# Rows of block 0 by selection products, block lists inside block 0, and activations turned inside a down product

## What is computed

```python
logits = (xt @ router_w + router_b)            # 512 x 32
top_val, top_idx = lax.top_k(logits, TOP_K)    # 4 of 32 experts for each token
gate = jax.nn.softmax(top_val, axis=-1)
# token/expert pairs are sorted by expert into groups padded to blocks of 128 rows
hh = xblk @ w1[e] + b1[e]                      # 128 x 1024 @ 1024 x 2048
glu = jnp.minimum(hh[:, :D_FF], SWIGLU_LIMIT)
lin = jnp.clip(hh[:, D_FF:], -SWIGLU_LIMIT, SWIGLU_LIMIT)
act = glu * jax.nn.sigmoid(SWIGLU_ALPHA * glu) * (lin + 1.0)
y = act @ w2[e] + b2[e]                        # 128 x 1024 @ 1024 x 1024
# y times its gate is added to the token's row; out = x_new + g_f * sum
```

## Time and profile before

| | |
|---|---|
| median of 3 runs | 2274.47 us (2274.46 to 2274.99) |
| the profiled execution | 2275.2 us, of which its span is 2273.4 us |
| TensorE busy | 2236.3 us (98% of the span), 10681 instructions |
| VectorE, ScalarE, GpSimd busy | 78%, 54%, 17% |
| the chain that ended last | 95% TensorE |
| DMA | 542.93 MB, mean 239 GB/s |
| granted TensorE clock, mean | 0.998 |

### The profile page before, as it was taken

How to read it: one execution, slowest core, us unless ns; L and a number is a source line. 1 busy time by engine, 2 the same in 40 slices (tenths; PEclk the granted TensorE clock), 3 DMA queues, 4 the chain that set the end, 5 groups by cost and what they waited for, 6 DMA issues and landing times.

```text
span 2273.4 us, 30491 instructions
## 1 busy us (share of the span) xinstructions
PE 2236.3 (98%) x10681; PEld 1829.3 (80%) x10681; DVE 1767.7 (78%) x1652; ACT 1238.2 (54%) x1154; POOL 378.3 (17%) x328
## 2 busy tenths in 40 slices
PE   7999999999999999999999999999999999999997
PEld 3888888888887887888788888888888888888886
DVE  6756665555656676757899999999999999999996
ACT  6322132222225524632777777777777777777774
POOL 3000000000221131101512121121112121212112
PEclk9999999999999999999999999999999999999999
DMA  8322323131321121246899999999999999999994
GB/s 301 121 93 93 103 83 130 59 135 57 103 93 38 38 75 38 59 149 224 314 358 371 373 366 382 382 372 362 386 364 373 371 364 383 377 368 380 378 370 168
DMA packets 135513, 542.93 MB, mean 239 GB/s; under 512 B 16131, under 2 KB 24467, under 8 KB 101390
## 3 DMA queue, kind: packets, MB, share of 16 engines
q1 hardware_dynamic: 123192, 516.30, 60.0%
q0 software_dynamic: 11952, 21.44, 4.0%
q10 hardware_dynamic: 296, 4.21, 0.5%
HBM read 533.79 MB, written 26.38 MB: 246 GB/s over the span
## 4 chain that ended last, share of the span: by engine, by line
PE 95%; DMA 1%; DVE 1%; POOL 1%; issue 1%; ACT 1%; POOLq 0%; SPq 0%; DVEq 0%; ACTq 0%
PE ps L2239 90%; PE ps L2795 1%; PE ps L2807 1%; PE ps L2586 1%; DMA ar<-h_d,ar 1%; POOL list_d L858 1%; DMA ar<-in_ctx 0%; PE ps L2531 0%; PE ps L2477 0%; DMA ar<-in_diff_lambda 0%; PE ps L2351 0%; DVE nmx L1846 0%; ACT hhi L1001 0%; PE ps L2684 0%; PE ps L2604 0%
## 5 line engine op out<-in xcount | busy, mean ns | idle before, releaser
L2239 PE MATMUL ps<-whi,yhi 128*128 128x512 f32 x1072 | 346.5, 393 | 0.1
L2239 PE MATMUL ps<-hhi,yhi 128*128 128x512 f32 x1072 | 342.6, 389 | 0.0
L2063 DVE TENSOR_TENSOR hlo<-raw,hhi 128x2048 fp32r<-128x2048 f32 x132 | 302.5, 2293 | 47.1 <-ACT hhi L1308 47.1
L1308 ACT ACTIVATE whi<-raw 128x2048 fp32r<-128x2048 f32 x132 | 253.4, 1920 | 99.1 <-PE ps L2239 99.1
L2063 DVE TENSOR_TENSOR wlo<-raw,whi 128x2048 fp32r<-128x2048 f32 x132 | 298.9, 2285 | 3.6 <-ACT whi L1308 2.0
L1308 ACT ACTIVATE hhi<-raw 128x2048 fp32r<-128x2048 f32 x132 | 253.1, 1918 | 76.3 <-PE ps L2239 76.3
L1421 DVE TENSOR_TENSOR wlo<-raw,whi 128x2048 fp32r<-128x2048 f32 x56 | 128.2, 2289 | 159.4 <-ACT whi L970 159.4
L2239 PEld LDWEIGHTS ps<-whi,yhi 128*128 128x128 f32 x1072 | 201.2, 188 | 53.9 <-issue 12.1
L2239 PEld LDWEIGHTS ps<-hhi,yhi 128*128 128x128 f32 x1072 | 201.2, 188 | 41.8
L2239 PE MATMUL ps<-whi,hhi 128*128 128x512 f32 x592 | 233.3, 394 | 0.0
L2239 PE MATMUL ps<-whi,hlo 128*128 128x512 f32 x592 | 230.9, 390 | 0.0
(11 more groups left out here) (354 smaller groups left out, 4251.8 us busy)
## 6 DMA issues: line engine op xcount, KB each, us to landing
raw<-in_exp_w SPq DMA_DIRECT2D x264, 1024.0 KB, 7.9
ar<-in_exp_w SPq DMA_DIRECT2D x132, 1024.0 KB, 7.8
raw<-in_w_in SPq DMA_DIRECT2D x44, 1024.0 KB, 5.1
raw<-in_w_mod SPq DMA_DIRECT2D x22, 1024.0 KB, 6.2
raw<-in_w_br_ret SPq DMA_DIRECT2D x8, 1024.0 KB, 5.2
ar<-in_x SPq DMA_DIRECT2D x8, 512.0 KB, 7.3
raw<-in_w_br_diff SPq DMA_DIRECT2D x4, 1024.0 KB, 5.1
raw<-in_w_out SPq DMA_DIRECT2D x4, 1024.0 KB, 9.9
```

The source lines that it names most:

```text
L1308: act.activation(e_whi[j % ESPL], e_raw[s], ACT.Copy).then_inc(e_hi, 1)
L2063: V.tensor_tensor(e_wlo[j % ESPL], e_raw[s], e_whi[j % ESPL].bitcast(F32), ALU.subtract).then_inc(e_lo, 1)
L2239: return pe.matmul(out, lhsT, rhs, start=start, stop=stop, skip_group_check=skip)
```

## The change

It has three parts.

First, the rows of block 0 are no longer gathered. TensorE makes them turned, as `ht` slices (the shifted rows of a token tile, still in SBUF) times the selection matrix: `direct_rows(t, q)`, four fp32 matmuls of 128x128 each, for four tiles and two banks. VectorE shifts tile 3's rows after `choose(3)`. As two of these tiles lie in raw slots 3 and 5, SyncE loads chunks 3 and 5 after the last of these products. The only early gather left is block 1's.

Second, the counts, the code lists, `first_rows` and the turned gates move from before `up(0)` into it (`route(kk)`, called after chunks 0, 2 and 3); bias parts follow chunks 4 to 7. The orders on ScalarE, VectorE and GpSimd are rewritten for it.

Third, `turn_act(i)` stands inside the down product of block i-1, after its third chunk of four, and the last down product goes to banks 2 and 3, its order by chunk first, with `act_high` and `act_low` of the last block by halves.

```diff
@@ SyncE
                 if t == LT - 1:
                     sp.dma_start(b2, a["exp_b2"]).then_inc(b2_loaded, 16)
-                if t == 2:
-                    sp.wait_ge(h2_stored, 16 * 2)
-                    load_w1(0, 0, RSLOTS + 1)
                 sp.wait_ge(n2_done, t + 1)
                 sp.dma_start(h2_d[t * P:(t + 1) * P, :], ht[t]).then_inc(h2_stored, 16)
             load_w1(0, 0, RSLOTS)
             sp.wait_ge(h2_stored, 16 * LT)
+            sp.wait_ge(xt_turned, 2)
             load_w1(0, 0, RSLOTS - 1)
+            load_w1(0, 0, RSLOTS + 1)
@@ GpSimd
-            list_tile(1, 0, 2)
+            list_tile(1)
+            list_tile(2)
+            list_tile(3, 0, 2)
             pool.wait_ge(first_ready, 1)
             pool.wait_ge(h2_stored, 16 * LT)
-            gather(firsti[:, 0, 0:1])
...
+            gather(firsti[:, 1, 0:1])
+            list_tile(3, 2)
@@ ScalarE (the lines between stay)
+            hi_e(0, 0)
             gate_exp(3)
-            hi_e(0, 0)
             hi_e(0, 1)
...
+            x_high(0)
             hi_e(0, 2)
-            x_high(0)
             hi_e(0, 3)
             act.wait_ge(b2_scaled, 1)
             act.activation(b23[0:32, :], b2, ACT.Copy).then_inc(gb_hi, 1)
...
@@ ScalarE, end
+            act_high(end, (0,))
             hi_e(end + 1, AHEAD)
-            act_high(end)
-            for j in range(AHEAD + 1, ESPL):
-                hi_e(end + 1, j)
+            act.wait_ge(e_used, chunk(end, MOE_N - 1) + 1)
+            act_high(end, (1,))
+            hi_e(end + 1, AHEAD + 1)
@@ VectorE
             pick_rows(2)
+            place(2)
+            choose(3)
             shift_rows(3)
-            choose(3)
-            gates_of(3)
             pick_rows(3)
...
             lo_e(0, 0)
...
             x_low(0)
-            for j in range(1, KH):
-                lo_e(0, j)
+            lo_e(0, 1)
+            lo_e(0, 2)
+            gates_of(3)
+            place(3)
+            dve.wait_ge(route_step, 1)
+            V.tensor_scalar(small[0:96, 0:1], ps[0:96, 0, 0:1], ...).then_inc(flag_ready, 1)
+            dve.wait_ge(route_step, 2)
+            firsti = first[:, :, :].bitcast(I32)
...
+            lo_e(0, 3)
+            V.tensor_tensor(b2, b2, F(A_GFB, D)[0:N_EXPERTS, :], ALU.mult).then_inc(b2_scaled, 1)
+            dve.wait_ge(route_step, 3)
...
             dve.wait_ge(bias_hi, 3)
...
+            lo_e(0, KH)
+            dve.wait_ge(route_step, 4)
...
@@ VectorE, end
+            act_low(end, (0,))
             give_y(end - 1, chunk(end, MOE_N - 1))
-            act_low(end)
+            act_low(end, (1,))
@@ TensorE
+            def direct_rows(t, q):
+                pe.wait_ge(pick_ready, t + 1)
+                pe.wait_ge(n2_done, t + 1)
+                for c in range(4):
+                    k = 4 * q + c
+                    last = mm(ps[:, q, c * P:(c + 1) * P], ht[t][:, k * P:(k + 1) * P], pick[:, t, 0, :],
+                              t == 0 and c == 0, t == LT - 1 and c == 3, True)
+                if t == LT - 1:
+                    last.then_inc(xt_turned, 1)
...
             turn_rows(3, 1)
-            keep_busy(2)
+            pe.wait_ge(route_ready, 1)
+            direct_rows(0, 0)
             logits(3, 1)
-            keep_busy(3)
-            first_rows(2)
+            direct_rows(0, 1)
+            direct_rows(1, 0)
+            direct_rows(1, 1)
             places(3)
-            keep_busy(2)
-            first_rows(3)
...
+            for t in range(2, LT):
+                for q in range(2):
+                    direct_rows(t, q)
+            def route(kk):
+                if kk == 0:
+                    pe.wait_ge(xt_lo, 2)
+                    pe.wait_ge(m_ready, 2 * LT)
+                    for t in range(LT):
+                        last = mm(ps[0:96, 0, 0:1], mask3[:, t, :], ones[:, 0:1], t == 0, t == LT - 1)
+                    last.then_inc(route_step, 1)
+                elif kk == 2:
+                    pe.wait_ge(dense_ready, LT)
+                    for t in range(LT):
+                        first_rows(t)
+                    pe.wait_ge(flag_ready, 1)
+                    mm(ps[0:96, 0, 0:1], tri[0:96, 0:96], small[0:96, 0:1], True, True).then_inc(route_step, 1)
+                elif kk == 3:
+                    pe.wait_ge(flag_ready, 2)
...
+                    pe.wait_ge(route_ready, LT)
+                    for t in range(LT):
+                        last = pe.transpose(ps[0:N_EXPERTS, 7, t * P:(t + 1) * P], dense[:, t, 2:2 + N_EXPERTS], ident)
+                    last.then_inc(route_step, 1)
@@ down, item
                     last.then_inc(e_used, 1)
+                    if k == MOE_N - FIRST - 2:
+                        between()
...
-                down(i - 1, i, FIRST)
-                turn_act(i)
+                down(i - 1, i, FIRST, lambda: turn_act(i))
-            pe.wait_ge(gathered, 16)
-            turn_x()
-            keep_busy(2)
+            pe.wait_ge(route_ready, LT - 1)
             pe.wait_ge(xt_lo, 1)
             def bias_part(kk):
-                t = kk - 3
-                if not 0 <= t < LT:
+                route(kk)
+                t = kk - KH
+                if t < 0:
                     return
@@ TensorE, end
-            pe.wait_ge(act_lo, end * 2 + 2)
-            pe.wait_ge(y_out, end + 1)
-            for c in range(2):
-                for k in range(MOE_N - FIRST):
+            for k, c in ((0, 0), (0, 1), (1, 0), (1, 1), (2, 0), (3, 0), (2, 1), (3, 1)):
+                if c == 0:
+                    if k % 2 == 0:
+                        pe.wait_ge(act_lo, end * 2 + k // 2 + 1)
+                    pe.wait_ge(e_lo, chunk(end + 1, k) + 1)
...
-                        o = ps[:, 6 + c, :]
+                    o = ps[:, 2 + c, :]
```

More of the change, by code:

```diff
@@ L950, in _ @@
             hold()
[L951 removed]
+            pool.wait_ge(gathered, n_items * 16 + 16)
             hold()
@@ L1321, in glu, with act_high @@
                 act.activation(F(A_GS, D), psf[:, 2 * COL:4 * COL], ACT.Silu, scale=ALPHA).then_inc(glu_done, 1)
-            def act_high(i):
-                for hf in range(2):
+            def act_high(i, halves=(0, 1)):
+                for hf in halves:
                     act.wait_ge(act_turned, i * 2 + hf + 1)
@@ L2164, in activate, with act_low @@
                                        op1=ALU.mult).then_inc(act_done, 1)
-            def act_low(i):
-                for hf in range(2):
+            def act_low(i, halves=(0, 1)):
+                for hf in halves:
                     dve.wait_ge(act_hi, i * 2 + hf + 1)
@@ L2208, in _ @@
                             ALU.subtract).then_inc(gb_lo, 1)
-            for j in range(KH, FIRST):
+            for j in range(KH + 1, FIRST):
                 lo_e(0, j)
@@ L2757, in _ @@
             turn_rows(3, 0)
-            first_rows(0)
             out_part(3, 1, 1)
-            first_rows(1)
             logits(3, 0)
@@ L2763, in _ @@
             turn_rows(3, 1)
-            keep_busy(2)
+            pe.wait_ge(route_ready, 1)
+            direct_rows(0, 0)
             logits(3, 1)
-            keep_busy(3)
-            first_rows(2)
+            direct_rows(0, 1)
+            direct_rows(1, 0)
+            direct_rows(1, 1)
             places(3)
-            keep_busy(2)
-            first_rows(3)
-            pe.wait_ge(m_ready, 2 * LT)
-            for t in range(LT):
-                last = mm(ps[0:96, 3, 0:1], mask3[:, t, :], ones[:, 0:1], t == 0, t == LT - 1)
@@ L2775, in _ @@
-            last.then_inc(route_step, 1)
-            keep_busy(1)
-            pe.wait_ge(flag_ready, 1)
-            mm(ps[0:96, 3, 0:1], tri[0:96, 0:96], small[0:96, 0:1], True, True).then_inc(route_step, 1)
-            keep_busy(1)
-            pe.wait_ge(flag_ready, 2)
-            oh = small[0:96, 8:8 + OVER + 2]
-            mm(ps[0:1, 3, 0:OVER + 2], cst[0:96, C_CODE:C_CODE + 1], oh, True, True)
-            mm(ps[0:1, 3, OVER + 2:2 * OVER + 4], cst[0:96, C_EXP:C_EXP + 1], oh, True, True)
@@ L2784, in _ @@
-            mm(ps[0:1, 3, 2 * OVER + 4:2 * OVER + 5], small[0:96, 0:1], ones[0:96, 0:1], True, True).then_inc(route_step, 1)
+            for t in range(2, LT):
+                for q in range(2):
+                    direct_rows(t, q)
[14 more added lines that the diff above has]
+                    pe.wait_ge(flag_ready, 2)
+                    oh = small[0:96, 8:8 + OVER + 2]
+                    mm(ps[0:1, 0, 0:OVER + 2], cst[0:96, C_CODE:C_CODE + 1], oh, True, True)
+                    mm(ps[0:1, 0, OVER + 2:2 * OVER + 4], cst[0:96, C_EXP:C_EXP + 1], oh, True, True)
+                    mm(ps[0:1, 0, 2 * OVER + 4:2 * OVER + 5], small[0:96, 0:1], ones[0:96, 0:1], True,
+                       True).then_inc(route_step, 1)
+                    pe.wait_ge(route_ready, LT)
+                    for t in range(LT):
```

(4 more changed lines are left out.)

96 lines of the change are left out of this document (37 added, 59 removed).

## The result

The changed kernel takes 2286.02 us (five executions, 2284.48 to 2286.87), the kernel before 2274.47; the recorded ratio, which is not simply that of the two medians (1.0051), is 1.0047 [1.0036, 1.0059]. It is slower, as forecast, but by 11.5 us where 6.0 were forecast, and outside the range of 2273.5 to 2284. Its profiled execution took 2284.48 us, with a span of 2282.7.

A forecast was written before the change was run, and what follows sets the result against it. TensorE, busy for 98% of the span and 95% of the chain, was taken as the bound. Block 0 +9.7, loop +0.5 and end -4.2 sum to +6.0 us: 2281.2 profiled, 2280.5 as a median, range 2273.5 to 2284.

The forecast's parts named there:

- Start of `up(0)`: Block 0: gather and fillers leave the path, so `up(0)` starts at 1081.1, 6.0 us earlier.
- Wait at chunk 3: Block 0: VectorE's low part of chunk 3 stands behind its wait for the first rows; TensorE idles 3.0 us.
- Wait at chunk 4: Block 0: ScalarE's high part of chunk 4 stands behind the turned gates' copies; TensorE idles 5.6 us.
- The table load: End of `up(0)`: load of 1.28 us and its activation of 0.2 fall behind the last bias part, formerly nearly hidden.
- Block 1: Start of block 1: 1127.7 against 1117.99, +9.7 us; without the clock's two falls +7.0.
- The clock's price: Block 0: half clock after both waits, 1.6 us each, bounds 0 and 1.6; rival that it stays up, chance 0.20.
- The loop: 32 blocks: splitting transposes from the bias costs +0.02 us per block, +0.5 in all.
- a hidden bias: Rival, loop: bias pairs run beside the long matmuls' drain, 0.25 us less per block, -8 over 32; chance 0.12.
- waiting activations: Rival, loop: TensorE idles in every block for late turned activations, 0.12 us each, +4 in all; chance 0.08.
- The end: Last down product starts near 2247.75 without idling, at 2.4 GHz: -4.2 us, up to 1.0 lost if TensorE's branches are exposed.
- the scatter of the block before: Rival, end: this scatter or the two last ones replace the wait, half of 4.2 us lost, 2282.6; chance 0.08.
- I took 0.7 off: Whole kernel: the median lies 0.7 us below the profiled execution, so 2281.2 profiled becomes 2280.5.

The follow-up runs named there:

- The two moves: Changed kernel with VectorE's chunk 3 low part before its first-rows wait: 2281.50 us; separately, with ScalarE's chunk 4 and 5 high parts before its bias and gate copies: 2277.88.
- block 0 alone: Changed kernel with its third part undone, so only the first two parts: 2285.89 us, ratio 1.0050 to the kernel before.
- the fillers: Changed kernel with 5 and 11 filler matmuls on TensorE inside the waits at chunks 3 and 4, nothing moved: 2283.34 us, ratio 1.0035 to the kernel before.
- the end alone: Kernel before with only the third part of the change: 2275.21 us, ratio 1.0001 to the kernel before.
- changed kernel with fillers ahead of the walk: Changed kernel with four TensorE fillers behind the last down product inside the loop, before the skipped passes: 2285.15 us, ratio 1.0046 to the kernel before.
- chunk 3's low part first: Changed kernel with VectorE's low part of chunk 3 ahead of its wait for the first rows: 2281.50 us, ratio 1.0030 to the kernel before.
- all-moves kernel with fillers in the wrong place: Changed kernel with chunk 3 low part, chunk 4 and 5 high parts, table load and second-bias scaling early, four fillers before the extra block: 2275.21 us, ratio 1.0005.
- all moves and the fillers ahead of the walk: Changed kernel with chunk 3 low part, chunk 4 and 5 high parts, table load, second-bias scaling early, four fillers behind the loop's last down product: 2273.23 us, ratio 0.9996.
- the end alone with the same fillers: Kernel before with only the third part, plus four TensorE fillers behind the last down product inside the loop: 2275.28 us, ratio 1.0004 to the kernel before.

## Why the prediction was right or wrong

**The direction and block 0.** Start of `up(0)`: 1081.1 forecast, 1081.24 seen. Wait at chunk 3: 3.0 forecast, 2.84 seen, put down to VectorE's low part. Wait at chunk 4: 5.6 forecast, 5.55 seen. The two moves showed that each is a line behind a wait for something else. The table load stood behind the last bias part, as forecast, but of the 1.5 us that were counted for it and its activation, moving it gave back only 0.3 of the turned activations' wait. Block 1: +9.7 forecast, +10.7 in the profile; block 0 alone gives +10.9 in the medians.

**The clock's price.** It fell at both places, as in the forecast. I took 1.6 each from the end of the kernel before. With the 0.5 that hides behind the second, this was 2.7 over a kernel without falls; the fillers showed 3.2 (2.4 and 0.8). I had written 1.6 as the upper bound of each, and it is not one. This term is mis-sized by 0.5, half of the 1.0 by which block 0 was missed.

**The loop.** +0.5 forecast, +0.6 seen (the last block's `turn_x` at 2246.19 in place of 2234.90 is +11.3, less the 10.7); 35.32 against the 35.30 of before. The 0.32 of the earlier trace rows for the step to 64 rows was the right price. The rule that a change of tiling mode drains the array (the Trainium skill, TensorEngine Tiling (Array Packing), Key Properties) agrees in sign with that row, 0.32 against 0.227 for a plain step; by the distance from block to block it cost no more here. The rivals of a hidden bias and of waiting activations are excluded by the same distance.

**The step that failed: "The end", -4.2 us, "TensorE hasn't idled, so it runs at 2.4 GHz".** In the profiled pair it gave -2.0, and in the medians nothing: the end alone 1.0001, and the changed kernel 2286.02 beside 2285.89 for block 0 alone. Three things were wrong in it.
- I read the 2.61 us of the earlier trace rows as a wait for VectorE. In that very trace VectorE's low part was done at 2249.37 (2248.09 + 1.28), TensorE's outer branch ran from 2246.2 to 2250.0, and the product started at 2250.32: the branch ended last. With VectorE's part moved ahead, 2.07 to 2.27 us of idle time were left. "Up to 1.0 of it is lost" was a bound with no row under it.
- So TensorE did idle, and its clock can fall as before. It did in the profile of the end alone.
- The forecast puts the last scatter 16.7 us behind the turned activations (2258.95 + 0.75 for VectorE's part + 0.97 from there to the scatter as before, less 2243.95). Behind GpSimd's chain it was never under 18.86, with or without idle time on TensorE. These 2.1 to 2.2 us are the whole miss in the profile. It was a rival, "the scatter of the block before" or the last two scatters, half of 4.2 lost, with a chance of 0.08. That its price came out right is partly luck, for the longer scatter in it was not foreseen: with the 6.35 us of before in place of 8.01 the chain would allow about 17.2 (an estimate), and 0.5 would have been lost.

**From the profile to the median.** I took 0.7 off; the changed kernel's median lies 1.5 above its profiled execution. Its executions fall into two groups, 2284.5 to 2284.7 and 2286.0 to 2286.9. The profile of the changed kernel with fillers ahead of the walk, whose executions form the same two groups (2284.7 to 2285.2, 2286.3 and 2286.5), is from the upper one (2286.34). It shows a third fall, behind the 1.70 us that the turned activations wait, which the changed kernel's profile (lower group) does not have:

```profile
1128.99 1.02 PE L2237 MATMUL ps<-hhi 64*128 64x512 f32 x4 [0.39 <-DVE yhi L2114]
...
1130.96 1.05 PE L2237 MATMUL ps<-whi,yhi 128*128 128x512 f32 x2
```

From block 1's bias to the last block's turned activations it is 1128.08 us there and 1126.55 in the changed kernel: 1.5 us. The same fall stands in two more profiles: in the kernel with chunk 3's low part first (0.50 in 1126 to 1128), and in the all-moves kernel with fillers in the wrong place (0.50 in 1120 to 1122, an execution of 2277.67 us where seven of 11 lie at 2275.0 to 2275.3). That it parts the changed kernel's own executions is likely, and not shown, since only one of them has a profile.

**The sum of the miss** (5.5 us): block 0 1.0, loop 0.1, end 2.2, profile to median 2.2. The last is as large as the end, and its cause is the one that stays open.

**A version without the loss.** With all moves and the fillers ahead of the walk it is 12.8 us under the changed kernel, and 1.6 us under the kernel before in the medians, which the interval (0.9987 to 1.0005) cannot tell from no change. Nine of its 11 executions lie within 0.5 us, where those of the kernel before spread from 2273.0 to 2275.9. That the fillers bring this steadiness is not shown: with the fillers in the wrong place seven of 11 lay within 0.4 us, and the end alone with the same fillers spread over 4.5.

## What to carry to other kernels

When small control work is moved inside a product, look at what each engine has queued behind the waits that come with it. Here two lines on VectorE and ScalarE cost 2.8 and 5.6 us, and in each case the next chunk's conversion could stand ahead of the wait. When a row names a releaser, compare the time at which that one was done with the end of the idle time; if they are far apart, look at the rows of the engine's own sequencer before moving the named work. And before a chain is shortened on one engine, work out how early the next engine in it can follow: here GpSimd's scatters would have given 2.0 us of the 4.2 at most.

## What was not expected of the hardware

- One branch at the end, over a loop that is not run, took TensorE's sequencer 2.2 to 3.9 us in 13 profiles and 0.35, 0.46 and 0.72 in three; a pass over a skipped block took 0.7. The same branches left no idle time in one kernel and 0.93 to 2.27 us in others that differ only elsewhere (0.93, 1.20, 1.90, 1.94, 1.95, 2.02, 2.07, 2.27), by how long the outer branch took.
- The indirect scatter of the block before took GpSimd 3.38 us with the third part and 1.58 or 1.59 without it, and 2.7 to 2.8 in most blocks of the loop. Why is open.
- In block 0 and at the end TensorE's granted clock fell to 0.50 behind every idle time of 2.6 us or more in these profiles, and behind some of the shorter ones: of two of 2.07 us one brought it, one didn't; 1.69 and 1.70 us ahead of block 1 did in two profiles and didn't in six; 1.38 us in one of three; 2.27, 2.02, 1.97 and 1.90 us did not. It also fell where no idle time was over 1 us, among the small products ahead of `up(0)`: 0.50 in 1072 to 1078 in the kernel with fillers in both waits, 0.53 in 1083 to 1085 in the end alone. A fall cost 0.7 to 2.4 us, by when it came and how much the next stage could absorb: the second one took 15.35 us from the bias to `turn_x` in the changed kernel and 16.44 in the same kernel with fillers at the end, against 14.54 without a fall.
